# Diffusion backbone step, modulation vectors: rounds 2 and 3 summed on VectorE, ScalarE and GpSimd, gate rows by transposes, two latent-key projections placed between them

## The chip, the cores and the metric

One core of a Trainium2 chip runs the kernel. The metric is device time in microseconds (us) of one execution. All data is float32.

## The reference, cut to what matters

```python
mod = jnp.einsum('bd,df->bf', jax.nn.silu(cond), P['w_ada'][l]) + P['b_ada'][l]     # 1024 -> 6144, for two conditions
sh1, sc1, g1, sh2, sc2, g2 = jnp.split(mod[:, None, :], 6, axis=-1)
h = rmsnorm(x, P['norm1_g'][l]) * (1 + sc1) + sh1
mix, ckv, krope = mixing(h, P, l, ctx)      # h @ w_in (1024 x 1440), then chunk MLP, pooling mixer, latent attention
x = x + g1 * mix
h = rmsnorm(x, P['norm2_g'][l]) * (1 + sc2) + sh2
x = x + g2 * ec_ffn(h, ...)                 # 16 experts, 1024 x 1024 matrices w1, w3, w2 each
```

There are 1024 tokens of the sample and 128 of the prompt. Each has its own condition vector (`c`, `c_ctx`), so each weight chunk of `w_ada` is used for two sums. The change touches only how `mod` is summed, how `g1` is spread over the partitions, and the place of two of the projections `h @ w_in`.

## The kernel before, in words

Each engine has its program written out by hand, and semaphores order them. The first 260 us work through a list `JOBS` (built by `plan_jobs`). A job is one use of a PSUM bank: TensorE (PE in the profile) fills the bank, and then VectorE ("D", DVE) or ScalarE ("A", ACT) evicts it. TensorE takes the jobs in order, VectorE its own in order, ScalarE its own in order. The banks are used in turn, eight of them, so a job can start only when the job eight places before it is evicted (`evicted(pe, BEFORE[n])`).

The modulation. `w_ada` is 1024 x 6144. It comes in 24 chunks of 1 MB, numbered 0 to 23, through a ring `ada_ring` of `RING` slots of 128 x 2048 in SBUF (`ada_chunk(n)` on SyncE's queue; the load of chunk n waits until chunk n - RING is used up). The four rounds (`ADA_ROUNDS`) give the shifts and scales of the first norm (rounds 0 and 1, chunks 0 to 7, on TensorE), g1 and sh2 (round 2, chunks 8 to 15) and sc2 and g2 (round 3, chunks 16 to 23). Each of rounds 2 and 3 ends in a job `("ada", r)`, whose result VectorE adds to the bias, and a job `("mod", r)`, four transposes into `modT`.

- Round 2 is summed on VectorE: `folded(n)` multiplies the 128 x 2048 chunk by one scalar for each partition and adds it to one sum for each condition (`fold[0]`, `fold[1]`), two instructions for each of eight chunks: L1697 for the first chunk, L1700 after it. They follow the eviction of the job `w_s`. `folded_products` (L654) then sums over the partitions on TensorE: eight matmuls.
- Round 3 is summed on TensorE (L644): each chunk is the moving operand of four matmuls. Four chunks (`ADA_AHEAD`) are taken ahead of the job `("ada", 2)`, four in the job `("ada", 3)`.
- The gate g1 is spread over the partitions by the four jobs `g1` (L725): a matmul of a one-hot row with `mod_rows`, 128 x 512 each.

Around them: the jobs `h` are the normalised rows transposed (L732), `va` and `u` projections evicted by ScalarE through GELU (L664, L629; L1404, L1407), `pin`, `ckv`, `cq` are projections of 8 matmuls each (L629). The job `("ckv", m, g)` is the latent key of feature block m, token group g. Before, the order at the place of the change is: `u` jobs, four chunks of round 3, `ada 2`, `mod 2`, four `g1`, `ada 3`, `pin (0,0)`, `mod 3`, five `pin`, then all six `ckv`. GpSimd (POOL) waits until round 3 has been used up, clears `pin`, and sums the pooling windows.

## Time and profile before

| | us |
|---|---|
| median of 3 runs | 1574.82 (1574.7 to 1578.1) |
| the profiled execution, its own time | 1575.8 |
| its span | 1574.0 |
| TensorE busy | 1544.3 (98%) |
| VectorE busy | 596.1 (38%) |
| ScalarE busy | 422.3 (27%) |
| GpSimd busy | 105.7 (7%) |

The span is the time from the first to the last instruction in the profile; the execution's own time is 1.8 us more. The granted TensorE clock is 0.999 of full over the span.

### The profile page before, as it was taken

The numbers are of one execution on the slowest core, as the hardware profiler recorded it, in microseconds if no ns is written. First come the engines' busy times: TensorE is split into PE (matmuls) and PEld (weight loads), VectorE is DVE, ScalarE is ACT, GpSimd is POOL, SyncE is SP. The second block draws the span as 40 slices with busy tenths as digits, with TensorE's granted clock in tenths as the row PEclk, the third lists the DMA queues.
The fourth block names the chain that finished last, engine by engine and source line by source line (L and its number), as shares of the span: only waits on it lengthen the run. The fifth ranks groups of instructions, "written<-read, shape, count | busy, mean of one in ns | idle before, by whom it ended". The sixth has DMA issues, their size and how long they took to land.

```text
span 1574.0 us, 26655 instructions
## 1 busy us (share of the span) xinstructions
PE 1544.3 (98%) x10753; PEld 1245.1 (79%) x10753; DVE 596.1 (38%) x1354; ACT 422.3 (27%) x965; POOL 105.7 (7%) x108
## 2 busy tenths in 40 slices
PE   6999999999999999999999999999999999999998
PEld 3744555666766666544699999999999999999997
DVE  2661545765756575125774111111111111111115
ACT  2400113555545453234520111101111111111114
POOL 0006200000000000111000000000000000000010
PEclk9999999999999999999999999999999999999999
DMA  9970002000010300352586878778787787877785
GB/s 372 348 267 6 30 7 60 8 21 7 0 27 0 127 2 1 116 191 92 189 293 256 309 255 305 269 266 307 253 310 263 263 297 267 312 249 270 288 280 215
DMA packets 122474, 291.05 MB, mean 185 GB/s; under 512 B 17651, under 2 KB 19226, under 8 KB 120238
## 3 DMA queue, kind: packets, MB, share of 16 engines
q1 hardware_dynamic: 117374, 271.85, 47.7%
q0 software_dynamic: 4752, 17.30, 4.1%
q8 instruction: 43, 0.70, 0.2%
q10 hardware_dynamic: 288, 1.05, 0.2%
q14 instruction: 17, 0.14, 0.0%
HBM read 266.18 MB, written 21.64 MB: 183 GB/s over the span
## 4 chain that ended last, share of the span: by engine, by line
PE 95%; DVE 2%; ACT 1%; issue 1%; DMA 0%; DVEq 0%; ACTq 0%
PE ps L1245 32%; PE ps L1277 16%; PE ps L877 9%; PE ps L629 8%; PE ps L978 7%; PE ps L926 5%; PE ps L911 4%; PE ps L664 2%; PE ps L831 2%; PE ps L843 1%; PE ps L856 1%; PE ps L644 1%; PE ps L1190 1%; PE ps L671 1%; PE ps L1200 1%; PE ps L732 1%
## 5 line engine op out<-in xcount | busy, mean ns | idle before, releaser
L1245 PE MATMUL ps<-mreg,wreg 128*128 128x144 f32 x4096 | 517.1, 286 | 0.0
L1245 PEld LDWEIGHTS ps<-mreg,wreg 128*128 128x128 f32 x4096 | 508.8, 190 | 0.7 <-ACT hreg L1563 0.4
L1277 PE MATMUL ps<-mreg,wreg 128*128 128x144 f32 x2048 | 266.3, 286 | 0.0
L1277 PEld LDWEIGHTS ps<-mreg,wreg 128*128 128x128 f32 x2048 | 258.1, 190 | 0.0
L2269 DVE TENSOR_TENSOR mreg<-ps,mreg 128x144 f32<-128x144 f32 x120 | 36.9, 308 | 429.6 <-PE ps L1245 429.5
L877 PE MATMUL ps<-wreg 128*128 128x512 f32 (+2 forms) x400 | 171.7, 519 | 0.2
L1600 ACT ACTIVATE mreg<-ps 128x144 f32<-128x144 f32 x128 | 37.1, 290 | 437.8 <-PE ps L1245 437.8
L978 PE MATMUL ps<-wreg,mreg 128*128 128x512 f32 x288 | 130.8, 598 | 0.0
L629 PE MATMUL ps<-hreg,wreg 128*128 128x512 f32 (+1 forms) x400 | 128.4, 479 | 0.0
L911 PEld LDWEIGHTS ps<-const,hreg 128*128 128x128 f32 x648 | 79.9, 141 | 58.8 <-issue 39.3
L1880 DVE TENSOR_REDUCE stat<-ps 128x1 f32<-128x1280 f32 (+1 forms) x72 | 97.7, 1358 | 57.2 <-PE ps L877 57.1
L629 PEld LDWEIGHTS ps<-hreg,wreg 128*128 128x128 f32 x400 | 64.6, 191 | 60.6 <-issue 60.2
L1439 ACT ACTIVATE hreg<-ps 128x512 f32<-128x512 f32 (+2 forms) x172 | 82.0, 502 | 102.0 <-PE ps L911 100.1
L1619 ACT ACTIVATE mreg<-ps,modT 128x128 f32<-128x128 f32 x128 | 47.0, 367 | 224.2 <-PE ps L1277 224.2
L1451 ACT ACTIVATE hreg<-ps,stat 128x1280 f32<-128x1280 f32 (+1 forms) x72 | 88.0, 1222 | 69.1 <-DVE stat L1882 69.1
L2173 DVE TENSOR_SCALAR mreg<-ps,gain,modT 128x128 f32<-128x128 f32 x112 | 45.8, 409 | 159.1 <-PE ps L1190 159.1
L911 PE MATMUL ps<-const,hreg 128*128 128x128 f32 x648 | 97.5, 274 | 0.0
L978 PEld LDWEIGHTS ps<-wreg,mreg 128*128 128x128 f32 x288 | 52.0, 190 | 54.1 <-issue 54.1
L926 PEld LDWEIGHTS ps<-hreg,wreg 128*64 128x64 f32 x1296 | 70.1, 137 | 22.6 <-ACT hreg L1439 15.3
L926 PE MATMUL ps<-hreg,wreg 128*64 128x128 f32 x1296 | 78.5, 275 | 0.9 <-ACT hreg L1439 0.9
L877 PEld LDWEIGHTS ps<-wreg 128*128 128x128 f32 x400 | 62.1, 190 | 15.5 <-issue 13.6
L1903 DVE TENSOR_SCALAR hreg<-hreg,stat 128x1280 f32<-128x1280 f32 (+1 forms) x72 | 60.2, 835 | 2.6
(310 smaller groups left out, 1182.7 us busy)
## 6 DMA issues: line engine op xcount, KB each, us to landing
wreg<-in_w_e_dram SPq DMA_DIRECT2D x96, 2048.0 KB, 12.2
wreg<-in_w_ada_dram SPq DMA_DIRECT2D x16, 1024.0 KB, 6.5
wreg<-in_w_ada_dram SPq DMA_DIRECT2D x16, 512.0 KB, 10.8
wreg<-in_x_sample_dram SPq DMA_DIRECT2D x8, 512.0 KB, 4.5
wreg<-in_w_out_dram SPq DMA_DIRECT2D x1, 4096.0 KB, 12.7
x_rows<-wreg SPq DMA_DIRECT2D x8, 512.0 KB, 3.0
xn_rows<-wreg SPq DMA_DIRECT2D x8, 512.0 KB, 2.9
wreg<-x_rows SPq DMA_DIRECT2D x8, 512.0 KB, 9.3
```

The costliest lines, as they stand in the source:

```text
L629: mm = pe.matmul(bank[BANK[n]][:, 0:gn], w_in_sb[:, k, w_at + m * P:w_at + (m + 1) * P], hT[:, k, g0:g0 + gn], start=(k == 0), stop=(k == ...
L877: mm = pe.matmul(bank[3 * (n % 2) + ch][:, 0:kn], qT[:, j, t * P:(t + 1) * P], kT[:, j, k0:k0 + kn], start=True, stop=True)
L911: mm = pe.transpose(bank[MID_BANK[("turn", n, ch)]][:, a * P:(a + 1) * P], prob[n % 2][:, kt * P:(kt + 1) * P], ident)
L926: mm = pe.matmul(pv_at(t)[64 * j:64 * j + 64, :], v_sb[:, kt, 64 * j:64 * j + 64], probT[:, 2 * (t % 2) + j, src * P:(src + 1) * P], start ...
L978: mm = pe.matmul(bank[o_bank(x)], mixT[:, k, t * P:(t + 1) * P], w_out_sb[:, k, hf * 512:(hf + 1) * 512], start=(k == 0), stop=(k == KD - 1))
L1245: mm = pe.matmul(o[:, 0:CAP], w[s][:, k, (f % 4) * P:(f % 4 + 1) * P], xsT[b][:, k, :], start=(k == 0), stop=(k == KD - 1))
L1277: mm = pe.matmul(bank[4 + dm % 2][:, 0:CAP], w2[f // 4][:, f % 4, dm * P:(dm + 1) * P], hidT[:, f, :], start=(f == 0), stop=(f == 7))
L1439: act.activation(probT[:, 2 * (t % 2) + j, ch * 512:ch * 512 + w], bank[MID_BANK[("turn", n, ch)]][:, 0:w], ACT.Copy).then_inc(t_out, 1)
L1451: act.activation(prob[n % 2][:, 0:w], src, ACT.Exp, bias=a_neg[:, n % 4:n % 4 + 1], scale=SCALE, accum_out=a_sum[:, n % 4:n % 4 + 1]).then ...
L1619: act.activation(yT[:, dm, :], bank[4 + dm % 2][:, 0:CAPS], ACT.Copy, scale=modT[:, 0, 40 + dm:41 + dm])
L1880: dve.tensor_reduce(a_max[:, r:r + 1], src, AX_X, ALU.max).then_inc(max_ok, 1)
L1903: dve.tensor_scalar(prob[n % 2][:, 0:w], prob[n % 2][:, 0:w], a_rec[:, r:r + 1], None, ALU.mult).then_inc(norm_ok, 1)
```

## The change

`RING` becomes 5. Round 3 is folded as round 2 is, so that TensorE has eight matmuls for it and not 32. For the second condition the work is split by columns: VectorE takes columns 0 to 639 (`POOL_FROM`), and of columns 640 to 2047 ScalarE multiplies a chunk by its scalar in place in the ring (`scaled`; the first chunk of a round straight into the sum), and GpSimd adds it to the sum. Where ScalarE does so among its evictions is the table `SCALED_AFTER`; where VectorE folds is `FOLDS_AFTER`: chunks 8 to 19 after `w_s`, 20 and 21 after `("ada", 2)`, 22 and 23 after `("mod", 2)`. The next load into a ring slot waits for VectorE, and for GpSimd's addition. `("ckv", 0, 0)` moves between `ada 2` and `mod 2`, and `("ckv", 1, 0)` behind `mod 2`. The gate is spread by 16 transposes of a `modT` column repeated 128 times. Chunks 8 to 12 are loaded ahead of the third part of `w_in`.

```diff
-RING = 6
+RING = 5
-ADA_AHEAD = 4
-ADA_DONE = (4, 8, 8 + ADA_AHEAD + 1, 17)
+POOL_FROM = 640
+SCALED_AFTER = {("u", 1, 0): (8,), ("va", 4): (9,), ("va", 5): (10,), ("va", 6): (11,), ("va", 7): (12,), ("va", 8): (13, 14),
+                ("u", 0, 1): (15, 16), ("u", 0, 2): (17,), ("u", 1, 1): (18, 19), ("u", 1, 2): (20, 21, 22, 23)}
+ADA_DONE = (4, 8, 9, 10)
+FOLDS_AFTER = {("w_s",): range(8, 20), ("ada", 2): (20, 21), ("mod", 2): (22, 23)}
...
-    jobs += [("ada", 2, "D"), ("mod", 2, "D")] + [("g1", c, hf, "D") for c in range(2) for hf in range(2)]
+    jobs += [("ada", 2, "D"), ("ckv", 0, 0, "D"), ("mod", 2, "D"), ("ckv", 1, 0, "D")]
+    jobs += [("g1", c, hf, "D") for c in range(2) for hf in range(2)]
...
-                if m in FOLDED:
-                    sp.wait_ge(fold_ok, SEL + 2 * (m - FOLDED[0]) + 2)
+                if m >= FOLD_FROM:
+                    sp.wait_ge(fold_ok, SEL + 2 * (m - FOLD_FROM) + 2)
+                    if m % KD:
+                        sp.wait_ge(pool_step, pool_added(m))
+                    else:
+                        sp.wait_ge(scaled_a, len(A_MODULATES) + m - FOLD_FROM + 1)
...
-            w_in_part(2)
+            for n in range(8, 12):
+                ada_chunk(n)
             sp.dma_start(ws_raw, w_s[0].rearrange("h p q -> p h q")).then_inc(small_in, 16)
...
-            for n in range(8, 24):
+            ada_chunk(12)
+            w_in_part(2)
+            for n in range(13, 24):
                 ada_chunk(n)
...
+            def folded_products(r):
+
+                o = bank[BANK[NUM[("ada", r)]]]
+                pe.wait_ge(fold_ok, SEL + 2 * (r - 1) * KD)
+                pe.wait_ge(pool_step, pool_added(ADA_ROUNDS[r][-1]))
...
-                if job[:-1] == ("ada", 2):
-                    evicted(pe, BEFORE[NUM[("ada", 3)]])
-                    ada_part(3, ADA_ROUNDS[3][0:ADA_AHEAD])
...
-                    row = 32 * hf + cnd
-                    mm = pe.matmul(o, ident[:, row:row + 1].to_broadcast([P, P]), mod_rows,
-                                   start=True, stop=True)
+                    if (cnd, hf) == (0, 0):
+                        evicted(pe, NUM[("mod", 2)])
+                    for a in range(4):
+                        k = 16 + 4 * hf + a
+                        mm = pe.transpose(o[:, a * P:(a + 1) * P], modT[:, cnd, k:k + 1].to_broadcast([P, P]), ident)
...
+            def scaled(n):
+
+                r, k = divmod(n - FOLD_FROM, KD)
+                part = ada_ring[n % RING][:, POOL_FROM:]
+                act.wait_ge(ada_in[n % RING], ada_there(n))
+                if k:
+                    act.wait_ge(fold_ok, SEL + 2 * (n - FOLD_FROM) + 1)
+                act.activation(part if k else fold[r][1][:, POOL_FROM:], part, ACT.Copy,
+                               scale=cond[:, k, 1:2]).then_inc(scaled_a, 1)
...
                 for cnd in range(2):
+                    z = 2048 if cnd == 0 else POOL_FROM
+                    acc = fold[r][cnd][:, 0:z]
                     if k == 0:
-                        ins = dve.tensor_scalar(fold[cnd], ada_ring[n % RING], cond[:, k, cnd:cnd + 1], None, ALU.mult)
+                        ins = dve.tensor_scalar(acc, chunk[:, 0:z], cond[:, k, cnd:cnd + 1], None, ALU.mult)
                     else:
-                        dve.wait_ge(fold_ok, SEL + 2 * k + cnd - 1)
-                        ins = dve.scalar_tensor_tensor(out=fold[cnd], in0=ada_ring[n % RING], scalar=cond[:, k, cnd:cnd + 1],
-                                                       in1=fold[cnd], op0=ALU.mult, op1=ALU.add)
+                        dve.wait_ge(fold_ok, SEL + 2 * (n - FOLD_FROM) + cnd - 1)
+                        ins = dve.scalar_tensor_tensor(out=acc, in0=chunk[:, 0:z], scalar=cond[:, k, cnd:cnd + 1],
+                                                       in1=acc, op0=ALU.mult, op1=ALU.add)
...
+            for n in range(FOLD_FROM, 3 * KD):
+                if n % KD:
+                    acc = fold[n // KD - 1][1][:, POOL_FROM:]
+                    pool.wait_ge(scaled_a, len(A_MODULATES) + n - FOLD_FROM + 1)
+                    then(pool.tensor_tensor(acc, acc, ada_ring[n % RING][:, POOL_FROM:], ALU.add))
             pool.wait_ge(ada_mm, ADA_DONE[3])
             pool.memset(pin, 0.0).then_inc(pool_cleared, 1)
```

TensorE at the place of the change, before (L644 is round 3, L654 the folded products of round 2, L720 `mod 2`, L725 the gate, L629 a projection):

```order
L629 MATMUL ps<-hreg,wreg 128x128 x8
L644 MATMUL ps<-wreg,cond 32x512 x16
L654 MATMUL ps<-mreg,vecs 32x512 x4
L654 MATMUL ps<-g_rows,vecs 32x512 x4
L720 MATMUL ps<-const,rt 128x128 x4
L725 MATMUL ps<-rt,const 128x512 x4
L644 MATMUL ps<-wreg,cond 32x512 x16
L629 MATMUL ps<-hreg,wreg 128x512 x8
```

The same place now (L670 folded products, L644 projections, L731 `mod 2`, L739 the gate):

```order
L644 MATMUL ps<-hreg,wreg 128x128 x8
L670 MATMUL ps<-mreg,vecs 32x512 x4
L670 MATMUL ps<-g_rows,vecs 32x512 x4
L644 MATMUL ps<-hreg,wreg 128x512 x8
L731 MATMUL ps<-const,rt 128x128 x4
L644 MATMUL ps<-hreg,wreg 128x512 x8
L739 MATMUL ps<-const,modT 128x128 x16
L670 MATMUL ps<-mreg,vecs 32x512 x4
L670 MATMUL ps<-wreg,vecs 32x512 x4
L644 MATMUL ps<-hreg,wreg 128x512 x8
```

Both blocks of sixteen matmuls are gone, the folded products stand there twice, and a projection stands on each side of `mod 2`.

VectorE after the last fold of round 2, before (L1733 evicts `ada 2`, L1745 `mod 2`, L1765 the gate, the last L1733 `ada 3`):

```order
L1700 SCALAR_TENSOR_TENSOR mreg<-wreg,cond,mreg 128x2048
L1700 SCALAR_TENSOR_TENSOR g_rows<-wreg,cond,g_rows 128x2048
L1733 TENSOR_TENSOR rt<-ps,creg 128x512
L1745 COPY modT<-ps 128x16 x2
L1765 COPY g_rows<-ps 128x512 x4
L1733 TENSOR_TENSOR rt<-ps,creg 128x512
```

And now, from the fold of chunk 19 on (L1729 folds, L1763 evicts `ada 2`, L1820 the two latent keys, L1775 `mod 2`):

```order
L1729 SCALAR_TENSOR_TENSOR mreg<-wreg,cond,mreg 128x2048
L1729 SCALAR_TENSOR_TENSOR wreg<-wreg,cond 128x640
L1763 TENSOR_TENSOR rt<-ps,creg 128x512
L1729 SCALAR_TENSOR_TENSOR mreg<-wreg,cond,mreg 128x2048
L1729 SCALAR_TENSOR_TENSOR wreg<-wreg,cond 128x640
L1729 SCALAR_TENSOR_TENSOR mreg<-wreg,cond,mreg 128x2048
L1729 SCALAR_TENSOR_TENSOR wreg<-wreg,cond 128x640
L1820 COPY creg<-ps 128x512
L1775 COPY modT<-ps 128x16 x2
L1729 SCALAR_TENSOR_TENSOR mreg<-wreg,cond,mreg 128x2048
L1729 SCALAR_TENSOR_TENSOR wreg<-wreg,cond 128x640
```

The evictions of `ada 2` and `mod 2` now stand behind the folds of chunks 16 to 19 and 20 to 21, and each second instruction of a fold has 640 columns and not 2048.

ScalarE between the last `va` and the last `u`, before (L1404 and L1407 are the GELU evictions):

```order
L1404 ACTIVATE mreg<-ps 128x256 x5
L1407 ACTIVATE mreg<-ps 128x512
L1407 ACTIVATE mreg<-ps 128x128
L1407 ACTIVATE mreg<-ps 128x512
L1407 ACTIVATE mreg<-ps 128x128
```

And now (L1428 and L1431 are those evictions, L1380 multiplies a chunk):

```order
L1380 ACTIVATE wreg<-wreg,cond 128x1408 x2
L1431 ACTIVATE mreg<-ps 128x512
L1380 ACTIVATE wreg<-wreg,cond 128x1408 x2
L1431 ACTIVATE mreg<-ps 128x128
L1380 ACTIVATE wreg<-wreg,cond 128x1408
L1431 ACTIVATE mreg<-ps 128x512
L1380 ACTIVATE wreg<-wreg,cond 128x1408 x2
L1431 ACTIVATE mreg<-ps 128x128
L1380 ACTIVATE wreg<-wreg,cond 128x1408 x4
```

Sixteen multiplications now stand among the evictions; the first of them, for chunk 8, stands ahead of ScalarE's eight evictions of `h` jobs. GpSimd has 14 additions of 128 x 1408 ahead of everything that it did before.

## Rows read from the trace of the kernel before

**Rows 1.** The page: busy time, and the chain that ended last.
```profile
PE   1544.3 (98%) x10753; PEld 1245.1 (79%) x10753; DVE 596.1 (38%) x1354; ACT 422.3 (27%) x965; POOL 105.7 (7%) x108
...
PE 95%; DVE 2%; ACT 1%; issue 1%; DMA 0%; DVEq 0%; ACTq 0%
```

**Rows 2.** Timeline of TensorE: start, duration, what [idle before <- releaser].
```profile
81.93 17.47 PE L629 MATMUL ps<-hreg,wreg 128*128 128x512 f32 x64
99.33 3.64 PE L644 MATMUL ps<-wreg,cond 128*32 128x512 f32 x32
102.79 1.04 PE L654 MATMUL ps<-mreg,vecs 128*32 128x512 f32 x8
103.65 1.04 PE L654 MATMUL ps<-g_rows,vecs 128*32 128x512 f32 x8
105.59 0.63 PE L720 MATMUL ps<-const,rt 128*128 128x128 f32 x4 [0.91 <-DVE rt L1733]
106.06 3.60 PE L725 MATMUL ps<-rt,const 128*128 128x512 f32 x8
109.59 3.64 PE L644 MATMUL ps<-wreg,cond 128*32 128x512 f32 x32
113.16 7.13 PE L629 MATMUL ps<-hreg,wreg 128*128 128x512 f32 x16
```

**Rows 3.** Timeline of VectorE: the folds of round 2 and the eviction behind them.
```profile
65.47 1.28 DVE L1697 TENSOR_SCALAR mreg<-wreg,cond 128x2048 f32<-128x2048 f32 x1
66.67 1.28 DVE L1697 TENSOR_SCALAR g_rows<-wreg,cond 128x2048 f32<-128x2048 f32 x1
67.86 2.35 DVE L1700 SCALAR_TENSOR_TENSOR mreg<-wreg,cond,mreg 128x2048 f32<-128x2048 f32 x1
70.12 2.35 DVE L1700 SCALAR_TENSOR_TENSOR g_rows<-wreg,cond,g_rows 128x2048 f32<-128x2048 f32 x1
...
97.27 2.35 DVE L1700 SCALAR_TENSOR_TENSOR g_rows<-wreg,cond,g_rows 128x2048 f32<-128x2048 f32 x1
104.76 0.69 DVE L1733 TENSOR_TENSOR rt<-ps,creg 128x512 f32<-128x512 f32 x1 [5.14 <-PE ps L654]
```

**Rows 4.** Timeline of ScalarE: SBUF to SBUF, of 1024 and of 512 columns.
```profile
45.41 1.04 ACT L1348 ACTIVATE g_rows<-mreg 128x1024 f32<-128x1024 f32 x1
...
152.53 0.63 ACT L1375 ACTIVATE mreg<-creg 128x512 f32<-128x512 f32 x1 [52.82 <-DVE creg L1790]
```

**Rows 5.** Timeline of GpSimd: its SBUF additions.
```profile
132.15 2.15 POOL L2427 TENSOR_TENSOR wreg<-wreg 128x1183 f32<-128x1183 f32 x1
...
142.12 2.69 POOL L2436 TENSOR_TENSOR wreg<-wreg 128x1184 f32<-128x1184 f32 x1
...
159.78 2.68 POOL L2435 TENSOR_TENSOR wreg<-wreg,mreg 64x1184 f32<-64x1184 f32 x1
162.54 3.02 POOL L2436 TENSOR_TENSOR wreg<-wreg 128x1184 f32<-128x1184 f32 x1
...
712.12 2.35 POOL L2445 TENSOR_TENSOR wreg<-wreg 128x1024 f32<-128x1024 f32 x1 [14.63 <-DVE wreg L1967]
```

**Rows 6.** Timeline of VectorE: instructions with two SBUF inputs, beside GpSimd and without it.
```profile
160.06 2.94 DVE L1677 TENSOR_TENSOR mreg<-mreg 128x512 f32<-128x512 f32 x1 [0.69 <-ACT mreg L1375]
...
175.04 0.69 DVE L1677 TENSOR_TENSOR mreg<-mreg 128x512 f32<-128x512 f32 x1 [0.70 <-ACT mreg L1375]
...
712.62 2.00 DVE L2062 SCALAR_TENSOR_TENSOR hreg<-wreg,creg 128x128 f32<-128x128 f32 x1
...
715.35 0.34 DVE L2062 SCALAR_TENSOR_TENSOR hreg<-wreg,creg 128x128 f32<-128x128 f32 x1
```

**Rows 7.** Timeline of TensorE: 16 transposes behind a wait, and 32 without one.
```profile
14.58 3.67 PE L732 MATMUL ps<-const,mreg 128*128 128x128 f32 x16 [4.69 <-DVE mreg L1687]
...
59.54 3.66 PE L732 MATMUL ps<-const,mreg 128*128 128x128 f32 x32
```

**Rows 8.** DMA issues up to 120 us: count, size, median us to landing.
```profile
wreg<-in_w_ada_dram SPq DMA_DIRECT2D x16, 1024.0 KB, 6.5
```

More of the change, by code:

```diff
@@ L66 @@
 ADA_ROUNDS = (range(0, 4), range(4, 8), range(8, 16), range(16, 24))
-FOLDED = ADA_ROUNDS[2]
-FOLDS = 2 * len(FOLDED)
+FOLD_FROM = ADA_ROUNDS[2][0]
 SEL = 3
-ADA_AHEAD = 4
-ADA_DONE = (4, 8, 8 + ADA_AHEAD + 1, 17)
+POOL_FROM = 640
[3 more added lines that the diff above has]
+FOLDS_AFTER = {("w_s",): range(8, 20), ("ada", 2): (20, 21), ("mod", 2): (22, 23)}
 PICKED = T + 1124
@@ L130, in plan_jobs @@
     q_sum = [("ssq", g, "D") for g in range(3)]
-    jobs += ckv[0] + [ckv[1][0], kv_sum[0], ckv[1][1]] + ckv[2] + [kv_sum[1], cq[0][0], kv_sum[2], gates[0]]
+    jobs += [ckv[1][0], kv_sum[0], ckv[1][1]] + ckv[2] + [kv_sum[1], cq[0][0], kv_sum[2], gates[0]]
     jobs += [cq[0][1], gates[1], cq[0][2], gates[2], cq[1][0], q_sum[0], gates[3], cq[1][1], gates[4], cq[1][2], gates[5]]
@@ L247, in build @@
         fin_squares = [view(mreg, s * D, D) for s in range(2)]
-        b_rows = view(creg, 0, 4, 512)
+        b_rows = view(creg, 384, 4, 512)
         ckvT = view(creg, 0, 2, ALLK)
@@ L296, in build @@
         wq_raw = view(xreg, 768, 3, P)
-        fold = [view(mreg, 4864, 2048), g1_rows[:].rearrange("p c d -> p (c d)")]
+        fold = [[view(mreg, 4352, 2048), g1_rows[:].rearrange("p c d -> p (c d)")],
+                [view(mreg, 2304, 2048), view(wreg, 21760, 2048)]]
         fold_sel = [vecs[:, 0:32], vecs[:, 32:64]]
@@ L331, in build @@
         inv_in, rope_in = sem("inv_in"), sem("rope_in")
-        mod_h_d, mod_h_a = sem("mod_h_d"), sem("mod_h_a")
+        mod_h_d, scaled_a = sem("mod_h_d"), sem("scaled_a")
         cleared, pool_cleared = sem("cleared"), sem("pool_cleared")
@@ L399, in ada_there, with pool_added @@
             return sum(32 if m < KD else 16 for m in range(n % RING, n + 1, RING))
+        def pool_added(n):
+            return n - FOLD_FROM - (n - FOLD_FROM) // KD
         def evicted(eng, n):
@@ L495, in _ @@
             evicted(sp, NUM[("h", 2, KD - 2)])
+            sp.wait_ge(ada_mm, ADA_DONE[3])
             sp.dma_start(inv_sb, inv_count.rearrange("p (m f) -> p m f", m=2)).then_inc(inv_in, 16)
-            sp.wait_ge(ada_mm, ADA_DONE[3])
             sp.dma_start(kr_mul, k_rope).then_inc(rope_in, 16)
@@ L646, in ada_part @@
                     mm.then_inc(ada_mm, 1)
-            def folded_products():
-                o = bank[BANK[NUM[("ada", 2)]]]
-                pe.wait_ge(fold_ok, SEL + FOLDS)
+            def folded_products(r):
+                o = bank[BANK[NUM[("ada", r)]]]
+                pe.wait_ge(fold_ok, SEL + 2 * (r - 1) * KD)
+                pe.wait_ge(pool_step, pool_added(ADA_ROUNDS[r][-1]))
                 for cnd in range(2):
                     for g in range(4):
-                        mm = pe.matmul(o[32 * g:32 * g + 32, :], fold_sel[cnd], fold[cnd][:, g * 512:(g + 1) * 512],
+                        mm = pe.matmul(o[32 * g:32 * g + 32, :], fold_sel[cnd], fold[r - 2][cnd][:, g * 512:(g + 1) * 512],
                                        start=(cnd == 0), stop=(cnd == 1))
@@ L661, in va_part @@
                     if t == 0:
-                        done, by = (mod_h_a, A_MODULATES) if k in A_MODULATES else (mod_h_d, D_MODULATES)
+                        done, by = (scaled_a, A_MODULATES) if k in A_MODULATES else (mod_h_d, D_MODULATES)
                         pe.wait_ge(done, by.index(k) + 1)
@@ L708, in _ @@
                         first_products()
-                    elif job[1] == 2:
-                        folded_products()
                     else:
-                        ada_part(3, ADA_ROUNDS[3][ADA_AHEAD:8])
+                        folded_products(job[1])
                 elif kind == "mod":
@@ L1400, in _ @@
                             act.activation(hT[:, k, 0:512], hT[:, k, 0:512], ACT.Identity, bias=modT[:, 0, k:k + 1],
-                                           scale=gain1[:, 0, k:k + 1]).then_inc(mod_h_a, 1)
+                                           scale=gain1[:, 0, k:k + 1]).then_inc(scaled_a, 1)
                         rows_rooted(1)
@@ L1423, in _ @@
                 a.then_inc(out_a, 1)
+                for chunk in SCALED_AFTER.get(job[:-1], ()):
+                    scaled(chunk)
             def keys_out(i):
@@ L1689, in folded @@
             def folded(n):
-                k = n - FOLDED[0]
-                if k == 0:
+                r, k = divmod(n - FOLD_FROM, KD)
+                chunk = ada_ring[n % RING]
+                if n == FOLD_FROM:
                     dve.wait_ge(cond_ok, 1)
@@ L1710, in _ @@
                     continue
+                for chunk in FOLDS_AFTER.get(previous, ()):
+                    folded(chunk)
+                previous = job[:-1]
                 if unsummed:
@@ L1726, in _ @@
                     dve.tensor_copy(wsT[:].rearrange("p h q -> p (h q)"), o).then_inc(out_d, 1)
-                    for chunk in FOLDED:
-                        folded(chunk)
                 elif kind == "ada":
```

4 lines of the change are left out of this document (2 added, 2 removed).

## The prediction

> **What bounds the kernel now.** I read the page first: TensorE is busy 98% of the span and makes up 95% of the chain that ended last [rows 1]. So what matters is what TensorE is handed at the place of the change, and whether it ever waits there. TensorE's timeline shows the place [rows 2]: the last `u` projections end at 99.33 us, then come four chunks of round 3, the folded products of round 2, one wait of 0.91 us for VectorE's eviction of `ada 2`, `mod 2`, the gate, the other four chunks, and at 113.16 the first `pin`. Apart from the 0.91 us it runs without a gap. VectorE's timeline shows why the fold of round 2 is hidden [rows 3]: it starts at 65.47, its sixteen instructions follow each other without a gap (2.26 us apart after the first two), and it ends at 99.6, while TensorE wants it at 102.8. That is a cover of only 3.2 us. Everything that follows asks whether the new fold, of twice as many chunks and on three engines, still fits.
>
> **What TensorE is spared.** Round 3's 16 + 16 matmuls take 102.79 - 99.33 = 3.46 and 113.16 - 109.59 = 3.57 us, together 7.03. Eight folded products come in their place: those of round 2 start 0.86 us apart for four, so 1.73. The gate's four matmuls take 109.59 - 106.06 = 3.53; sixteen transposes cost 16 x 0.11 (3.66 us for 32 [rows 7]) = 1.76. The wait at `mod 2` goes, since a projection stands there: from the second four products to `mod 2` are 1.94 us, of which 0.87 is work, so 1.07. Sum: 5.30 + 1.77 + 1.07 = 8.1 us less on TensorE [rows 2]. The two latent-key projections are only moved, about 6.97 us each (7.13 with the tail of the last one). If the fold keeps up, that is the gain.
>
> **What a chunk of the fold costs each engine.** VectorE: the 2048 columns of the first condition, 2.26 us. For 640 columns no row stands; from 0.34 us for 128 columns [rows 6] and 2.35 for 2048 [rows 3] a line gives 0.88, less the 0.09 by which successive ones overlap, 0.79. So 3.05 us for a chunk. The first chunk of a round takes 1.20 and, in proportion, some 0.45. ScalarE: 1408 columns from 0.63 us for 512 and 1.04 for 1024 [rows 4], 1.35 us. GpSimd: an addition of 1408 columns. The rows give 2.69 us for 1184 columns of two tiles and 2.35 for 1024, both 2.3 ns a column, and 2.15 for 1183 columns where both inputs are one tile, 1.8 ns [rows 5]. The new addition has two tiles and writes on one input, as L2445 does, so I take 2.3 ns: 3.22 us; bounds 2.56 (1.8 ns) and 3.6 (2.55 ns, from the 3.02 us of the last row with 1184 columns). If the three ran side by side, the pace would be some 3.1 to 3.3 us for a chunk against 4.52 before, and it would fit.
>
> **They don't run side by side.** This is the step on which the forecast rests. VectorE's addition L1677 of 512 columns with both inputs in SBUF takes 0.69 us at 175.04, but 2.94 at 160.06. GpSimd's addition L2435 lasts from 159.78 to 162.46; VectorE's ends at 163.00, so it did its half microsecond of work only when GpSimd had ended. It happens again with the very instruction of the fold: a SCALAR_TENSOR_TENSOR of 128 columns takes 0.34 us at 715.35 and 2.00 at 712.62, ending at 714.62, just after the GpSimd addition that lasts from 712.12 to 714.47. The other direction shows too: GpSimd's L2436 starts at 162.54, while VectorE's L1677 is doing its work, and takes 3.02 us and not 2.69 [rows 5, 6]. So an instruction of VectorE with two SBUF inputs and an addition of GpSimd exclude each other for their whole length. The Trainium skill states this as a rule (SBUF — State Buffer, section Who interferes with whom): a VectorE instruction with two SBUF inputs contends with a GpSimd one that reads SBUF, and whichever comes second fully blocks; the trace agrees. Without that rule and these rows the sum would be the 8.1 us of gain, less a small wait.
>
> Fourteen of VectorE's folds for each condition, and all of GpSimd's additions, are of these kinds. The cost of a chunk is then a sum, 3.05 + 3.22 = 6.27 us, and not a maximum; before it was 4.52.
>
> **Round 2.** From 65.47: 1.65 for chunk 8; 7 x 3.05 = 21.4 for VectorE; 7 x 3.22 = 22.5 for GpSimd; and one instruction of chunk 16 (1.2) that gets in before the last addition, since ScalarE's 1.35 us lies between. The sum of round 2 is ready at 112.2. TensorE comes for it at 99.33 (the four chunks of round 3 that stood there are gone). It waits 12.9 us. The ring doesn't bound this: a slot is free after GpSimd's addition, a chunk lands 6.5 us after its issue [rows 8], and five slots at 6.3 us leave over 20 us. ScalarE's `va` and `u` evictions are late behind `scaled`, but none is wanted until the gate's jobs take their banks.
>
> **Round 3.** What is left after 112.2: 0.45 + 21.4 + 22.5 = 44.4 us, and about 1.4 where VectorE evicts or GpSimd waits for ScalarE and neither uses the port. So it is ready at 158.0. TensorE meanwhile: folded products to 113.9, `ckv (0,0)` to 120.8, then it waits for the eviction of `ada 2`, which stands on VectorE behind chunk 19, done at about 128.3; `mod 2` to 129.4, `ckv (1,0)` to 136.3; the gate, behind `mod 2`'s eviction (behind chunks 20 and 21), to about 144; then `ada 3` from 158.0 to 159.7. Before, TensorE was at the first `pin` at 113.16 [rows 2]; now at 159.7, with 2 x 6.97 of `ckv` already done: 159.7 - 13.9 - 113.2 = **32.6 us later**.
>
> **After the wait.** The only long wait of TensorE that the rows show in the opening is 4.69 us; 16 transposes behind it take 3.67 us, as long as 32 do later [rows 7], though the granted clock reads full. I add that loss of 1.8 us once, for the last and longest wait; behind the earlier waits it is hidden in the next one. Later stages keep their order and wait on nothing that is nearer than before: the loads of `inv_count` and the sums of the pooling windows move with the first `pin`, and are wanted over 60 us later. So 34.4 us on the profiled execution's own 1575.8, 1610.2; the median is 1.0 lower, so **1609 us**.
>
> **Rivals.** *(a) It keeps up, faster.* If the two engines shared the port at little cost (against it: all three delayed instructions above), VectorE would end chunk 19 near 99.3, `ada 2` would be ready in time, and only the last chunk would be late: VectorE's part of 23 at 115.0, ScalarE to 116.4, GpSimd to 119.8, TensorE there at 117.0. Gain 8.1 - 2.6 = 5.5, so 1569. It decides at a pace below 4.2 us for a chunk (33.9 us for eight). Chance 0.13. *(b) Cheaper additions.* With 2.56 us each the fourteen save 9.2 us: 1600; with 3.6 they cost 5.3 more: 1614. Both are inside my case. *(c) VectorE keeps the port as long as it has chunks*, and GpSimd gets in only when the ring runs dry; the rows show no GpSimd addition waiting before a row of such folds. Then chunk 14 waits for the addition of chunk 9 and its 6.5 us landing; round 2 is ready near 115, but the total on the port is the same and the end near 157 to 160: 1608 to 1611. *(d) The exclusion is only partial*, say half of GpSimd's time hidden: 14 x 1.6 us less, 1587. Chance 0.08. *(e) No change*: only if wait and saving cancel, 0.03. My case with (b) and (c): 0.76.
>
> **How the numbers follow.** My case spans 1598 to 1617: the two bounds of the addition, and 3 us of further gaps. To hold 8 in 10 the range goes down into (d): 1588 to 1619. A difference of 0.2%, some 3 us, is about what this measurement can tell. Faster 0.13, same 0.03, slower 0.84.
>
> **What would show it.** In the changed profile: VectorE's folds of 2048 columns at 2.35 us alone but many rows of 4 to 6 us; GpSimd's fourteen additions with a pitch near 6.3 us, or in bursts with VectorE waiting; waits of TensorE before the folded products of some 13 us each, and one of 8 us before `mod 2`, ended by VectorE; the first `pin` near 160 us; everything behind it as before. I am wrong if the folds stay at 2.35 us while GpSimd adds: then the first `pin` comes near 119 us. ScalarE's multiplication of chunk 8 ahead of the `h` evictions could cost TensorE some tenths, no more.

## The result, and the profile after

The changed kernel takes 1641.03 us (median, 1640.22 to 1641.68), the kernel before 1575.26 us in the same comparison: ratio 1.0414, 95% interval 1.0401 to 1.0427. It is slower, as forecast, but by 65.8 us and not by 34: 1641 lies above the whole range of 1588 to 1619. The profiled execution took 1640.22 us.

From the page of the changed kernel: busy times; the instruction queue; the chain that ended last; the busiest group with its idle time.
```profile
PE 1559.4 (95%) x10713; PEld 1258.2 (77%) x10713; DVE 649.2 (40%) x1370; ACT 444.2 (27%) x981; POOL 161.9 (10%) x122
...
q8 instruction: 88, 1.44, 0.4%
...
PE 88%; DVE 7%; issue 3%; ACT 1%; DMA 0%; POOL 0%; DVEq 0%; ACTq 0%; POOLq 0%
...
L1258 PE MATMUL ps<-mreg,wreg 128*128 128x144 f32 x4096 | 525.4, 289 | 16.7 <-issue 16.7
```
Against [rows 1], VectorE's part of the chain has gone from 2% to 7%, which fits the forecast waits, and "issue" (idle time of an engine that waits for nothing the profile shows) from 1% to 3%, which the prediction did not have. The last line is the expert products of a loop that stands some 900 us behind the fold, with 16.7 us of idle time that no engine ends.

Timeline of TensorE of the changed kernel, the stretch that answers to [rows 2]. L670 are the folded products, L731 `mod 2`, L739 the gate, L644 the projections, L770 the sums of squares.
```profile
81.95 17.47 PE L644 MATMUL ps<-hreg,wreg 128*128 128x512 f32 x64
110.48 1.93 PE L670 MATMUL ps<-mreg,vecs 128*32 128x512 f32 x8 [11.06 <-POOL g_rows L2452]
...
114.05 7.67 PE L644 MATMUL ps<-hreg,wreg 128*128 128x512 f32 x16
...
126.43 1.08 PE L731 MATMUL ps<-const,rt 128*128 128x128 f32 x4 [4.71 <-DVE rt L1763]
...
139.10 3.57 PE L739 MATMUL ps<-const,modT 128*128 128x128 f32 x16 [2.32 <-DVE modT L1775]
155.07 1.93 PE L670 MATMUL ps<-mreg,vecs 128*32 128x512 f32 x8 [12.40 <-POOL wreg L2452]
...
158.64 7.56 PE L644 MATMUL ps<-hreg,wreg 128*128 128x512 f32 x16
...
212.51 1.10 PE L770 MATMUL ps<-mreg,const 128*128 128x512 f32 x2 [3.54 <-DVE mreg L1703]
```
The four waits stand where the prediction placed them: 11.1, 4.7, 2.3 and 12.4 us. The first `pin` starts at 158.64.

Timeline of VectorE: L1726, which starts the second condition's sum of round 2; folds of chunks 9 to 11; and L1726 again for round 3.
```profile
66.69 0.55 DVE L1726 TENSOR_SCALAR g_rows<-wreg,cond 128x640 f32<-128x640 f32 x1
...
69.41 0.88 DVE L1729 SCALAR_TENSOR_TENSOR g_rows<-wreg,cond,g_rows 128x640 f32<-128x640 f32 x1
70.21 2.35 DVE L1729 SCALAR_TENSOR_TENSOR mreg<-wreg,cond,mreg 128x2048 f32<-128x2048 f32 x1
72.47 3.80 DVE L1729 SCALAR_TENSOR_TENSOR g_rows<-wreg,cond,g_rows 128x640 f32<-128x640 f32 x1
76.19 5.25 DVE L1729 SCALAR_TENSOR_TENSOR mreg<-wreg,cond,mreg 128x2048 f32<-128x2048 f32 x1
81.37 0.87 DVE L1729 SCALAR_TENSOR_TENSOR g_rows<-wreg,cond,g_rows 128x640 f32<-128x640 f32 x1
...
107.25 3.44 DVE L1726 TENSOR_SCALAR wreg<-wreg,cond 128x640 f32<-128x640 f32 x1
```
Timeline of GpSimd, the additions of the fold.
```profile
71.14 8.15 POOL L2452 TENSOR_TENSOR g_rows<-g_rows,wreg 128x1408 f32<-128x1408 f32 x2 [70.70 <-ACT wreg L1380]
83.15 8.10 POOL L2452 TENSOR_TENSOR g_rows<-g_rows,wreg 128x1408 f32<-128x1408 f32 x2 [3.85 <-ACT wreg L1380]
...
107.04 3.29 POOL L2452 TENSOR_TENSOR g_rows<-g_rows,wreg 128x1408 f32<-128x1408 f32 x1 [3.85 <-ACT wreg L1380]
...
151.78 3.15 POOL L2452 TENSOR_TENSOR wreg<-wreg 128x1408 f32<-128x1408 f32 x1 [3.85 <-ACT wreg L1380]
```
A fold of 640 columns takes 0.88 us or 3.80, one of 2048 columns 2.35 or 5.25. The difference is 2.9 us both times, whatever the width, so it is not work but a wait inside the instruction, for the addition of GpSimd that runs meanwhile. The last row shows more than the prediction said: L1726 has only one SBUF input, and it too takes 3.44 us and not 0.55 beside the addition of 107.04. The row at 71.14 also shows the other direction: two additions, of which one by itself takes 3.15 us (151.78), span 8.15; the first begins while VectorE's fold of 70.21 still has 1.4 us to go. Two chunks cost 83.15 - 71.14 = 12.0 us, 6.0 for each.

**Where the 64.4 us of span come from** (1638.4 against 1574.0), by the starts of matching rows in the two traces. The first `pin`: 158.64 - 13.9 of projections already done - 113.16 [rows 2] = +31.6. From there to 619 us in the kernel before: +4.3, of which 3.5 is the wait at 212.51 and 0.4 a slower first `pin`. Between 796 and 814 us, most of it in the unread products ahead of the router: +2.7. In the expert stage: +25.9. The first of the four was forecast as 32.6. For the other three, 32.9 us, the forecast had 1.8.

The wait at 212.51 (VectorE's timeline, L1703 being the square that L770 sums; then GpSimd's, its pooling window sums):
```profile
204.51 4.77 DVE L1839 SCALAR_TENSOR_TENSOR creg<-creg,vT,rt 128x512 f32<-128x512 f32 x2
...
210.57 1.79 DVE L1703 TENSOR_TENSOR mreg<-mreg 128x512 f32<-128x512 f32 x1 [0.70 <-ACT mreg L1399]
```
```profile
205.70 3.03 POOL L2470 TENSOR_TENSOR wreg<-wreg,mreg 64x1184 f32<-64x1184 f32 x1
208.81 3.01 POOL L2471 TENSOR_TENSOR wreg<-wreg 128x1184 f32<-128x1184 f32 x1
```
The same exclusion once more: the last window sum ends at 211.82 (208.81 + 3.01), and the square, 0.69 us alone [rows 6], ends at 212.36. The window sums start behind the last `pin` in both kernels. The sums of squares stand behind the `ckv` projections, and two of those, 14 us, have gone ahead. So the sums come closer to the window sums.

The unread products (L638, matrix products whose result nobody reads; L623 in the kernel before), TensorE's timeline of the changed kernel:
```profile
801.51 0.61 PE L1046 MATMUL ps<-quad_sum,creg 128*128 128x16 f32 x2 [0.41 <-DVE creg L2035]
801.96 2.91 PE L638 MATMUL ps<-const 128*128 128x256 f32 x6
...
804.87 2.77 PE L638 MATMUL ps<-const 128*128 128x256 f32 x6
```
And of the kernel before, the same place:
```profile
765.26 0.40 PE L1033 MATMUL ps<-quad_sum,creg 128*128 128x16 f32 x2 [0.41 <-DVE creg L2005]
765.50 1.54 PE L623 MATMUL ps<-const 128*128 128x256 f32 x6
```
Half the rate, and it is the clock: the windows below. The pauses ahead of them (0.33 and 0.41 us) are the same in the kernel before, where the products run at the full rate.

The expert stage: TensorE's timeline, the first products of the second turn of its loop; then that line's entry in the list of waits (total, times, longest).
```profile
1066.32 5.86 PE L1258 MATMUL ps<-mreg,wreg 128*128 128x144 f32 x32 [3.44 <-issue]
```
```profile
PE ps L1258 <- issue: 16.7, 5, 3.5
```
The loop over the experts (two in a turn, six turns) stops 3.1 to 3.5 us at each of its five returns to its start, and the 32 products behind take up to 5.86 us and not 4.09. The granted clock of TensorE says why. Windows of the changed kernel (the window, its length, busy time and instructions of each engine, then granted clock, DMA share, GB/s): behind the second wait for a folded sum, behind the loop's return in three pieces, and at the unread products.
```profile
155.10:157.00 1.90, 1.90 (x12) 0.62 (x16) 1.90 (x4) 0.00 (x0) 0.00 (x0) 0.50 0.05 9
...
1066.40:1068.00 1.60, 1.60 (x11) 1.60 (x12) 0.00 (x0) 0.00 (x0) 0.00 (x0) 0.84 1.03 415
1068.00:1070.00 2.00, 2.00 (x10) 2.00 (x10) 0.00 (x0) 0.29 (x1) 0.00 (x0) 0.50 1.04 418
...
1071.50:1073.00 1.50, 1.50 (x15) 1.50 (x14) 0.66 (x2) 0.00 (x0) 0.00 (x0) 1.00 1.04 423
802.00:804.60 2.60, 2.60 (x7) 1.92 (x8) 1.08 (x6) 1.81 (x4) 0.00 (x0) 0.50 0.67 202
```
The clock is at its lower level, 0.50 (1.2 of 2.4 GHz), for some microseconds, and then back at 1.00. Behind the 12.4 us wait it is low at once; behind the loop's return the first products still run at 1.00, which is why the first window reads 0.84. A turn takes 102.4 to 103.1 us, before 97.65. The queue `q8 instruction` moves 8 or 9 packets of 16 KB in a turn; in the kernel before, between none and 5.

### The profile page after: what moved, and what is told of

The parts are those of the page before. It is cut to its first block, busy times and chain, and to the rows that moved or that the text cites. A ratio compares the mean times of both kernels' runs of the same rounds, so it can differ in the third digit from the quotient of the medians.

```text
span 1638.4 us, 26667 instructions
## 1 busy us (share of the span) xinstructions
PE 1559.4 (95%) x10713; PEld 1258.2 (77%) x10713; DVE 649.2 (40%) x1370; ACT 444.2 (27%) x981; POOL 161.9 (10%) x122
## 4 chain that ended last, share of the span: by engine, by line
PE 88%; DVE 7%; issue 3%; ACT 1%; DMA 0%; POOL 0%; DVEq 0%; ACTq 0%; POOLq 0%
PE ps L1258 31%; PE ps L1290 15%; PE ps L890 9%; PE ps L991 7%; PE ps L644 5%; PE ps L939 5%; PE ps L924 4%; DVE mreg L1729 3%; PE ps L844 1%; PE ps L856 1%; PE ps L869 1%; PE ps L1203 1%; PE ps L687 1%; PE ps L1213 1%; PE ps L680 1%
## 5 line engine op out<-in xcount | busy, mean ns | idle before, releaser
L1258 PE MATMUL ps<-mreg,wreg 128*128 128x144 f32 x4096 | 525.4, 289 | 16.7 <-issue 16.7
L1290 PE MATMUL ps<-mreg,wreg 128*128 128x144 f32 x2048 | 266.3, 287 | 0.0
L644 PE MATMUL ps<-hreg,wreg 128*128 128x512 f32 (+1 forms) x400 | 132.2, 489 | 0.0
L644 PEld LDWEIGHTS ps<-hreg,wreg 128*128 128x128 f32 x400 | 66.0, 195 | 64.1 <-issue 61.8
L2503 POOL DMA_INDIRECT x_rows<-hreg,idx_s x15 | 23.9, 1591 | 537.8 <-DVE mreg L2203 522.6
## 6 DMA issues: line engine op xcount, KB each, us to landing
wreg<-in_w_out_dram SPq DMA_DIRECT2D x1, 4096.0 KB, 12.9
```

The source lines that it names most:

```text
L644: mm = pe.matmul(bank[BANK[n]][:, 0:gn], w_in_sb[:, k, w_at + m * P:w_at + (m + 1) * P], hT[:, k, g0:g0 + gn], start=(k == 0), stop=(k == ...
L1258: mm = pe.matmul(o[:, 0:CAP], w[s][:, k, (f % 4) * P:(f % 4 + 1) * P], xsT[b][:, k, :], start=(k == 0), stop=(k == KD - 1))
L1290: mm = pe.matmul(bank[4 + dm % 2][:, 0:CAP], w2[f // 4][:, f % 4, dm * P:(dm + 1) * P], hidT[:, f, :], start=(f == 0), stop=(f == 7))
```

## The experiments

My theory of the expert stage before any run: the loop (1668 instructions of TensorE in the built program) is moved 80 instructions towards the start by the change, and then lies on one block of 256 more than TensorE keeps, so each turn fetches code again. (The pages bear out the 80: 40 matmuls and 40 weight loads fewer. A turn has 800 of each in the trace.) Rivals: the folding in the opening changed the loads' rhythm, or SBUF traffic of the other engines. And for the opening: mutual exclusion of VectorE and GpSimd against simple overload.

**1. 80 instructions ahead of the changed kernel's jobs.** 160 waits come out as 80 instructions (26747 on the page and not 26667).
```
+            for _ in range(160):
+                pe.wait_ge(cleared, 1)
             for n, job in enumerate(JOBS):
```


> The changed kernel with 160 waits that are always fulfilled (80 instructions) at the very start of TensorE's program, where it waits 9.5 us for a load anyway. They put every later instruction of TensorE where it stood in the kernel before; nothing else changes. Theory 1, the five pauses of 3.4 us at the turns of the expert loop (and the half-rate stretch behind each, 5.3 us together) come from where the loop's instructions lie: the pauses go, the expert loop takes 97.7 us a turn again, and the time is 1641 less 26, some 1615 us. Theory 2, they come from the later start of the loop (its loads, its phase against the clock): the pauses stay, 1641 us.

Measured: 1613.32 us (1612.58 to 1614.4), ratio to the kernel before 1.0236 (1.0219 to 1.0253). From its page:
```profile
q8 instruction: 43, 0.70, 0.2%
...
L1260 PE MATMUL ps<-mreg,wreg 128*128 128x144 f32 x4096 | 517.1, 286 | 0.0
```
The same computation, 80 useless instructions more, 27.7 us faster. Neither rival can do this, since the loads and the work of the other engines are the same. The five pauses are gone, their half-rate stretches too (517.1 us busy against 525.4), and so is the half rate at 802 us. The fetched code is what it was before the change, 0.70 MB. The placement of the loop is the cause of 25 us (16.7 of pauses and 8.3 of products at the lower clock). The other 2.7 us are the unread products, and that the 80 instructions did this is not shown: the times of one kernel lie in groups that far apart from one execution to the next (experiments 5 to 8).

**2. 128 instructions ahead of the kernel before.** The same edit with `range(256)`, in the kernel that had no pauses.

> The kernel before with 256 waits that are always fulfilled (128 instructions) at the very start of TensorE's program. Theory 1 (where the loop's instructions lie): a shift by 128 instructions, half of a fetched block of 256, puts the loop of 1668 instructions across one block more, as the change did with a shift of 80 the other way: five pauses appear, 1575 plus 26, some 1601 us. Theory 2 (the later start): no pauses, 1575 to 1578 us.

Measured: 1615.62 us (1608.25 to 1618.56), ratio 1.0235 (1.0203 to 1.0267). Waits of TensorE:
```profile
PE ps L1247 <- issue: 24.2, 5, 5.0
PE ps L701 <- issue: 14.7, 1, 14.7
```
Pauses appear in the untouched algorithm, five of them, 89 packets. Their size was missed: 4.7 to 5.0 us and not 3.4. With 12.3 us more of busy time (529.4 against 517.1) they make 36.5 us of the 41.5 by which this trace's span is longer. The four executions lie 10 us apart, so the sizes hold for the one that was traced. Another 4.1 are the 128 waits themselves, which last until 14.7 us and outlast the loads that cover them.

**3. The fold on VectorE alone**: no multiplication on ScalarE, no addition on GpSimd.
```
-POOL_FROM = 640
+POOL_FROM = 2048
...
-                for chunk in SCALED_AFTER.get(job[:-1], ()):
-                    scaled(chunk)
...
-                    then(pool.tensor_tensor(acc, acc, ada_ring[n % RING][:, POOL_FROM:], ALU.add))
```


> The changed kernel, but VectorE folds all 2048 columns for both conditions, and ScalarE's 16 multiplications and GpSimd's 14 additions are gone (same sums). Theory A, VectorE and GpSimd exclude each other: every fold takes 2.35 us, 4.52 us a chunk; round 2 is ready at 99.6, and round 3 at about 137 and not 155; the first pin projection starts near 139 and not 158.6, so some 20 us less than the changed kernel, 1621 us with the pauses of the expert loop. Theory B, the longer queue of VectorE is what costs, and the helpers help: later than 158.6, over 1641.

Measured: 1618.26 us (1616.19 to 1620.27), ratio 1.0261 (1.0242 to 1.0279). TensorE's timeline:
```profile
116.26 1.08 PE L726 MATMUL ps<-const,rt 128*128 128x128 f32 x4 [7.58 <-DVE rt L1756]
...
135.12 1.93 PE L665 MATMUL ps<-mreg,vecs 128*32 128x512 f32 x8 [7.12 <-DVE wreg L1722]
...
138.69 6.70 PE L640 MATMUL ps<-hreg,wreg 128*128 128x512 f32 x14
```
The first `pin` comes 20 us earlier than with two helpers. Every two-input fold takes 2.34 or 2.35 us. The helpers take 34% of VectorE's columns off it (1408 of 4096 in a chunk) and make the whole 20 us later. The pauses in the expert loop are there too (16.4 us), since TensorE's program is nearly the same.

**4. GpSimd writes the same columns but reads nothing**: a fill with zeros in place of the addition. This kernel leaves that part of the sums out.
```
-                    then(pool.tensor_tensor(acc, acc, ada_ring[n % RING][:, POOL_FROM:], ALU.add))
+                    then(pool.memset(acc, 0.0))
```


> The changed kernel, but GpSimd writes zeros over its columns of the second condition's sum in place of adding (a part of the sum is so left out). GpSimd then reads nothing of SBUF. Theory A (exclusion is between VectorE's second SBUF input and GpSimd's reads): VectorE's folds take 2.35 and 0.88 us each, the first pin projection starts near 119 us, and the time is some 38 to 40 us under the changed kernel, about 1602. Rival (any work of GpSimd holds VectorE, reads or not): folds are still held by the 1.3 us of each write; the first pin projection starts near 130 us, about 1613.

Measured: 1603.57 us (1598.24 to 1603.87), ratio 1.0161 (1.0139 to 1.0182). VectorE's, GpSimd's and TensorE's timelines:
```profile
69.97 2.34 DVE L1729 SCALAR_TENSOR_TENSOR mreg<-wreg,cond,mreg 128x2048 f32<-128x2048 f32 x1
72.24 0.88 DVE L1729 SCALAR_TENSOR_TENSOR g_rows<-wreg,cond,g_rows 128x640 f32<-128x640 f32 x1
```
```profile
70.88 1.27 POOL L2452 MEMSET g_rows<- 128x1408 f32 x1 [70.43 <-ACT wreg L1380]
```
```profile
119.27 3.27 PE L644 MATMUL ps<-hreg,wreg 128*128 128x512 f32 x7
```
The fill lies inside the fold and the fold keeps its 2.34 us. The fill is also shorter (1.27 us), so the run by itself doesn't price an addition that overlaps. It shows that GpSimd's writing does not hold VectorE, and what the order of jobs is worth when nothing is held: the first `pin` at 119.27, where the prediction put it for that case, 7.8 us ahead of the kernel before (8.1 forecast). That lead is gone by the time the expert products begin, at 776.0 us and in the kernel before at 775.4: the 3.5 us wait at the sums of squares and the slow unread products are in this trace too. So even with nothing held in the fold and without the loop's pauses this kernel would have gained nothing here.

**5 to 8. The parts without the fold.** The gate by transposes, with `g1` behind `ada 3`:
```
-    jobs += [("ada", 2, "D"), ("mod", 2, "D")] + [("g1", c, hf, "D") for c in range(2) for hf in range(2)]
+    jobs += [("ada", 2, "D"), ("mod", 2, "D"), ("ada", 3, "D")] + [("g1", c, hf, "D") for c in range(2) for hf in range(2)]
```


> The kernel before with one part of the change: the gate by 16 transposes of modT columns, its four jobs behind ada 3 so that the second half of round 3 lies over mod 2's eviction. TensorE has 1.77 us less work; its program is 17 instructions longer, not enough to bring the expert loop onto one block more. Expected 1573.7 us. If the transposes cost what the matmuls did, or the wait for mod 2 shows, 1575.5.

One projection, `ckv (0,0)`, between `ada 2` and `mod 2`:
```
-    jobs += [("ada", 2, "D"), ("mod", 2, "D")] + [("g1", c, hf, "D") for c in range(2) for hf in range(2)]
+    jobs += [("ada", 2, "D"), ("ckv", 0, 0, "D"), ("mod", 2, "D")] + [("g1", c, hf, "D") for c in range(2) for hf in range(2)]
```


> The kernel before with one projection, ckv (0,0), between ada 2 and mod 2 (and the bias rows moved by 384 columns, a wait for the weights ahead of it). The 0.9 to 1.1 us wait before mod 2 goes: 1574.4 us. Rival: the first sum of the latent keys comes 7 us nearer to GpSimd's window sums, and the wait of 3.5 us that the changed kernel shows at L770 (VectorE's two-input instructions held by GpSimd) appears in part: 1575.5 to 1578.

Both:

> The two parts together on the kernel before, round 3 left on TensorE and no GpSimd addition: 1.77 and 1.07 us less, 1572.7 us; with the wait of the rival of the run before, up to 1576.

Both, and `cq (0,0)` ahead of the second sum of squares (`[cq[0][0], kv_sum[1], kv_sum[2], ...]`):

> As the run before, but cq (0,0) ahead of the second sum of the latent keys, which gives VectorE 7 us more before TensorE wants its sum of squares. If the held two-input instructions make a wait there, it goes: 1572.7 us, the fastest of the four. If there was none, the same time as the run before.

Measured, against 1575.61 us of the kernel before: gate 1576.25, ratio 1.0007 (0.9996 to 1.0017); projection 1576.16, 0.9999 (0.999 to 1.0007); both 1572.96, 0.9982 (0.9973 to 0.9991); both with `cq` 1573.03, 0.9981 (0.9972 to 0.999). In its trace the gate alone meets a load that has not landed:
```profile
108.73 1.06 PE L644 MATMUL ps<-wreg,cond 128*32 128x512 f32 x8 [0.63 <-DMA wreg<-in_w_ada_dram]
```
That doesn't explain its median: this execution, with the 0.63 us in it, took 1573.93 us. With the projection alone the wait ahead of `mod 2` is gone in the trace, but the unread products run at half rate (2.91 us for six), and this execution took 1577.08 us. The times lie in groups. Of 35 executions of the kernel before, 28 took 1574.5 to 1576.6 us and seven 1577.4 to 1578.4; with the projection alone it was six at 1574.0 to 1575.3 and six at 1577.1 to 1577.8, a distance near the 2.7 us of the half rate; with the gate alone four took 1573.9 to 1575.0 and the others up to 1580.9. Within the lowest groups the median is 1575.4 for the kernel before, 1574.5 with the projection (forecast 1574.4) and 1574.2 with the gate (forecast 1573.7, and 0.6 of load on top). So each part probably gains about what was forecast, but groups picked afterwards don't prove it, and the medians of all executions show no gain. Together the two edits gain 2.6 us, against 2.8 forecast in the prediction for gate and wait (1.77 + 1.07): faster than the kernel before by 0.18% (0.09 to 0.27). The rival named with the projection alone, a wait at the sum of the latent keys, is not borne out: it is 0.5 us, as in the kernel before, so moving `cq` had nothing to gain here.

**9 to 11. Where the loop stands**: 40, 256 and 336 instructions ahead of the changed kernel's loop. 40 stand at the start as in the first run; 256 stand half ahead of each of the two long waits for the folded sums (here too two waits make one instruction); 336 are these and the 80 of the first run.
```
             def folded_products(r):
 
                 o = bank[BANK[NUM[("ada", r)]]]
+                for _ in range(256):
+                    pe.wait_ge(cleared, 1)
```


> The changed kernel with 80 waits that are always fulfilled, 40 instructions, at the start of TensorE's program, so that its expert loop starts 40 instructions later and not 80. Theory: the program is fetched in blocks of 256 instructions (the Trainium skill, Runtime: NRT & Kernel Launch, Instruction fetch mechanics), and what matters is only where in a block the loop starts. 40 lies between 0, with five pauses, and 80, with none, so here the theory allows either all five pauses or none, 1641 or 1613 us, but nothing between: q8 88 packets or 43. Rival: the pauses grow with the distance moved, then about half of them or pauses of half the length, near 1627 us.

> The changed kernel with 256 fulfilled waits, 128 instructions, ahead of each of the two long waits of TensorE for the folded sums (11.1 and 12.4 us), so that they are hidden there or nearly so. The expert loop starts 256 instructions later, a whole block. Theory: same place in a block as in the changed kernel, so five pauses of 3.4 us, q8 about 88 packets, 1641 us and up to 3 us more at each of the two waits. Rival: what counts is how far along the loop starts; 80 later made the pauses go, so they are gone here too, 1613 us.

> As the run with 256 instructions, with 80 more at the start of TensorE's program as in the run that lost its pauses: the loop starts 336 instructions later, a block and 80. Theory: no pauses, q8 about 45 packets, 1613 us and up to 3 us more at each of the two waits. Rival: pauses come as soon as the loop is moved away from where it was in the kernel before (80 earlier and 128 later both had them), so they are here too: 1640 us or more.

Measured: 1657.91 us (1657.5 to 1658.32); 1637.53 (1636.93 to 1638.13); 1613.7 (1612.92 to 1614.47). The group of the expert products on the page of each, then the first pauses of the run with 40 and of the run with 256:
```profile
L1260 PE MATMUL ps<-mreg,wreg 128*128 128x144 f32 x4096 | 528.9, 290 | 32.3 <-issue 32.3
```
```profile
L1260 PE MATMUL ps<-mreg,wreg 128*128 128x144 f32 x4096 | 519.5, 287 | 16.3 <-issue 16.3
```
```profile
L1262 PE MATMUL ps<-mreg,wreg 128*128 128x144 f32 x4096 | 517.1, 286 | 0.0
```
```profile
1064.55 1.86 PE L1260 MATMUL ps<-mreg,wreg 128*128 128x144 f32 x13 [3.33 <-issue]
1069.73 4.04 PE L1260 MATMUL ps<-mreg,wreg 128*128 128x144 f32 x19 [3.32 <-issue]
```
```profile
1064.28 4.18 PE L1260 MATMUL ps<-mreg,wreg 128*128 128x144 f32 x32 [3.30 <-issue]
1069.53 0.27 PE L1215 MATMUL ps<-const,mreg 128*128 128x128 f32 x1 [1.06 <-issue]
```
256 more has the pauses, 336 more has none, and 80 more had none: whether there are pauses goes by the position modulo 256, and "further along" and "away from the place of before" both fall. 40 more went beyond what either theory said: two pauses in a turn, ten in all, 32.3 us, and 11.8 us more of busy time than without pauses. I had allowed "either all five pauses or none"; the number of pauses depends on the position within a block too. The run with 256 is not an exact copy of the changed kernel either. Behind four of its five pauses a second one of 1.0 to 1.3 us follows (4.5 us in all, at L1215), and behind those four the products run at the full clock (4.18 us), where the changed kernel's slow ones take 5.58 to 5.86 and no second pause shows.

The second pauses tell where the blocks end. They come 13 products into the loop with 40 instructions more, and 32 products in with 256 more: 19 products and their weight loads are 38 instructions, close to the 40 by which the starts differ. From this I estimate that the changed kernel's loop starts some 64 instructions ahead of the end of a block. Its 1668 instructions then lie on eight blocks, and so they do with 40, 256 and 208 more (experiment 2); with 80 and 336 more they start some 16 instructions into a block and fit on seven. By this estimate the runs with pauses are those with eight blocks, and none of the others pauses.

**12. The wait at 212.51.** The kernel of the first run with `cq (0,0)` ahead of the second sum of squares:
```
-    jobs += [ckv[1][0], kv_sum[0], ckv[1][1]] + ckv[2] + [kv_sum[1], cq[0][0], kv_sum[2], gates[0]]
+    jobs += [ckv[1][0], kv_sum[0], ckv[1][1]] + ckv[2] + [cq[0][0], kv_sum[1], kv_sum[2], gates[0]]
```


> The changed kernel without the pauses (80 instructions ahead, as in the first run), and the first query-latent projection cq(0,0) placed ahead of the second key-latent sum of squares instead of behind it. Theory: the 3.5 us wait of TensorE at that sum is there because VectorE's squares are held by GpSimd's pooling window sums, which last till 211.8 us; seven us of work ahead of it cover it. The wait goes, 1613.3 - 3.5 = 1609.8 us. Rival: the wait only moves to the next product that VectorE feeds, 1613 us.

Measured: 1609.5 us (1609.15 to 1610.18) beside 1613.32 of the first run. In its list of waits the longest one of the sums is gone:
```profile
PE ps L772 <- DVE mreg L1705: 0.5, 1, 0.5
```
The wait goes, and the gain of 3.8 us is close to the 3.5 expected. The traces show that other rows moved as well: the first run lost 1.7 us more behind its wait (8.73 us for a projection, 7.03 in the changed kernel) and this one has six of the unread products at half rate (2.91 us). So the total agrees, but not every part of it is the wait.

## Why the prediction was half right

- **Mutual exclusion** ("They don't run side by side"): right, and the pace was 6.0 us for a chunk, forecast 6.27. The two additions that stand by themselves take 3.15 and 3.29 us (forecast 3.22), ScalarE's multiplication 1.47 (1.35), a fold of 640 columns 0.88 (0.88). VectorE and GpSimd alternate in pairs of chunks and not chunk by chunk; whether that makes the last 0.2 us is not shown. Experiment 3 prices it: with the two helpers the first `pin` comes 20 us later than with none. The rule of the Trainium skill, SBUF — State Buffer, section Who interferes with whom, which holds for a GpSimd instruction that reads SBUF, is borne out on both sides: the additions hold (2.9 us), the fills of experiment 4 do not.
- **Rounds 2 and 3**: forecast waits 12.9, about 8, then the end of the gate near 144 and 14 us for `ada 3`; measured 11.1, 4.7, 2.3 (gate done at 142.7) and 12.4. The first `pin` was forecast at 159.7 and came at 158.64: 32.6 us late forecast, 31.6 measured. Rival (d), half of GpSimd's time hidden, is out.
- **Half rate after the wait**: forecast once, 1.8 us behind the first `pin`, taken from [rows 7]. It came, but as a lower clock (0.50), and ahead of the first `pin`: the two rows of folded products take 1.93 and 1.96 us there and not 1.04 each. These 1.8 us are inside the 158.64; behind it only 0.4 us more are lost. The stretch of [rows 7] reads 1.00, so what slowed it was something else, not known here, that happened to have the size.
- **The failed step** is the sentence "Later stages keep their order and wait on nothing that is nearer than before", and with it the term of the sum for everything behind the first `pin`: 1.8 us forecast, 32.9 measured. The prediction gave no row for it and never asked what fewer instructions on TensorE do to a loop behind them. The order was kept and it was still wrong, in three ways. The sums of squares had come 14 us nearer to GpSimd's window sums, 3.5 us (experiment 12). The unread products ran at half rate in the traced execution, 2.7. And the expert loop, whose code no diff line touches, began to pause at each return, 25 us (shown by experiments 1, 2 and 9 to 11 to follow from where it starts; that the pause is a fetch of code is read from the queue's 8 or 9 packets in a turn).
- **The sum**: 34.4 forecast. 31.6 + 4.3 + 2.7 + 25.9 = 64.5 of span. Without the pauses (experiment 1) the kernel is at 1613.3, inside the range; without the wait at the sums (experiment 12) at 1609.5, beside a forecast of 1609. That agreement is partly luck: 1.0 us too much for the fold and the misplaced 1.8 stand against 1.8 us behind the first `pin` that were not forecast, 1.4 of them in the unread products.

Open: why the pause at the loop's return takes 3.4 us in one position and 4.9 in another, and exactly where within a block the pauses begin. The distances tried, counted from the changed kernel's loop: 0 pauses once in a turn, 256 once with a short second one, 40 twice, 208 (experiment 2) once and longer, 80 (also the kernel before) and 336 not at all, nor experiments 5 to 8 with 1 to 18 instructions more than the kernel before. Open too is what decides the half rate of the unread products: in the traces they ran at full rate in the kernel before and in experiments 1, 2, 5 and 8 to 11, and at half rate, wholly or for the first six, in the changed kernel and in 3, 4, 6, 7 and 12. Not tried is a version with ScalarE as the only helper.

## What to carry to other kernels

A helper engine is worth its columns only if its instructions and those of the engine it helps don't exclude each other: read, in the trace of before, one instruction of each kind beside the other and alone, and add their times where they exclude each other. When a change alters the number of instructions ahead of a large loop on the engine that bounds the kernel, look at idle time "issue" at the loop's return and at the instruction queue's packets; a few dozen instructions more or less can be worth more than the change. And a job that is moved ahead takes its time away from where it was cover: where it stood, a wait can appear.
